# High and low activations side by side: 512 moving columns into two halves of a bank in the third mixer and the cross attention

## The reference

```python
h = rms_norm_2(x, g_mix[i])
q, k, v, z, xbc, dt_raw = jnp.split(h @ w_in[i], splits, axis=-1)
attn = dilated_attention(...q, k, v...)           # 16 heads of 64
ssm = ssd_mixer(z, xbc, dt_raw, ...)              # conv, silu, chunked scan, gate
x = x + jnp.concatenate([attn, ssm], axis=-1) @ w_out[i]
...
q = (h @ w_q)                                     # 4 heads of 128
kv = (mem_h @ w_kv)                               # keys and values of 256 memory rows
p = jax.nn.softmax(jnp.einsum('bshd,bmhd->bhsm', q, k), axis=-1)
```

## Time and profile before

| | |
|---|---|
| median of 3 runs | 3293.85 us (3293.05 to 3294.2) |
| the profiled execution, its own time | 3295.74 us |
| its span in the profile | 3293.9 us |
| PE, matmuls busy | 3277.0 us, 99% of the span |
| DVE busy | 2168.9 us, 66% |
| ACT busy | 1543.6 us, 47% |
| third mixer and cross attention, from its first piece to its last | 2014.8 to 2549.7 us of the span |

### The profile page before, as it was taken

The page is one execution under the profiler, slowest core; times in us unless marked ns, Lnnn a source line. Parts: engine busy times, 40 slices in busy tenths (PEclk is TensorE's granted clock), DMA queues, the critical chain, the costliest instruction groups (busy, mean ns, idle before and its releaser), DMA issues.

```text
span 3293.9 us, 40488 instructions
## 1 busy us (share of the span) xinstructions
PE 3277.0 (99%) x16298; PEld 2765.5 (84%) x16298; DVE 2168.9 (66%) x1803; ACT 1543.6 (47%) x1550; POOL 188.7 (6%) x272
## 2 busy tenths in 40 slices
PE   8999999999999999999999999999999999999999
PEld 7888888888888888888888888999889888888887
DVE  6565777777676565776777676577776555555555
ACT  6645444443445654444444445347554534444443
POOL 0101000000000000000000000000030000000000
PEclk9999999999999999999999999999999999999999
DMA  7456777777755445867777754444354455555554
GB/s 282 154 179 226 267 261 252 249 251 260 254 198 196 171 167 210 276 242 268 252 252 247 263 201 164 154 141 143 140 204 147 173 192 191 186 185 189 191 191 166
DMA packets 106523, 686.28 MB, mean 208 GB/s; under 512 B 14065, under 2 KB 16145, under 8 KB 29617
## 3 DMA queue, kind: packets, MB, share of 16 engines
q1 hardware_dynamic: 84128, 591.43, 50.0%
q0 software_dynamic: 22288, 93.31, 9.2%
HBM read 640.81 MB, written 2.10 MB: 195 GB/s over the span
## 4 chain that ended last, share of the span: by engine, by line
PE 98%; DVE 1%; DMA 1%; ACT 0%; issue 0%; POOL 0%; DVEq 0%
PE ps L528 27%; PE ps L530 27%; PE ps L529 27%; PE ps L496 3%; PE ps L497 3%; PE ps L498 3%; PE ps L550 2%; DVE w_lo L1765 1%; PE ps L633 0%; PE ps L622 0%; PE ps L678 0%; DMA gain_rows_sb<-in_gain_rows 0%; PE ps L592 0%; PE ps L899 0%; PE ps L910 0%; PE ps L949 0%
## 5 line engine op out<-in xcount | busy, mean ns | idle before, releaser
L1187 ACT ACTIVATE w_hi<-w_raw 128x2048 fp32r<-128x2048 f32 x558 | 1067.7, 1915 | 1231.2 <-DMA w_raw<-in_weights 1231.0
L1765 DVE TENSOR_TENSOR w_lo<-w_raw,w_hi 128x2048 fp32r<-128x2048 f32 x558 | 1277.3, 2296 | 480.3 <-ACT w_hi L1187 477.6
L528 PE MATMUL ps<-w_hi,actb_hi 128*128 128x512 f32 x1920 | 749.2, 390 | 0.0
L530 PE MATMUL ps<-w_lo,actb_hi 128*128 128x512 f32 x1920 | 747.1, 389 | 0.0
L529 PE MATMUL ps<-w_hi,actb_lo 128*128 128x512 f32 x1920 | 747.0, 389 | 0.0
L528 PE MATMUL ps<-w_hi,h_hi 128*128 128x512 f32 x1216 | 474.9, 391 | 0.0
L530 PE MATMUL ps<-w_lo,h_hi 128*128 128x512 f32 x1216 | 473.2, 389 | 0.0
L529 PE MATMUL ps<-w_hi,h_lo 128*128 128x512 f32 x1216 | 473.1, 389 | 0.0
L1845 DVE TENSOR_TENSOR x_stream<-x_stream,ps 128x1024 f32<-128x1024 f32 x160 | 195.4, 1221 | 348.9 <-PE ps L530 346.4
L530 PEld LDWEIGHTS ps<-w_lo,actb_hi 128*128 128x128 f32 x1920 | 360.4, 188 | 74.9
L528 PEld LDWEIGHTS ps<-w_hi,actb_hi 128*128 128x128 f32 x1920 | 360.5, 188 | 73.9
(11 more groups left out here) (380 smaller groups left out, 3137.8 us busy)
## 6 DMA issues: line engine op xcount, KB each, us to landing
w_raw<-in_weights SPq DMA_DIRECT2D x558, 1024.0 KB, 4.8
gate_rows<-in_conv_rows POOLq DMA_DIRECT2D x20, 1024.0 KB, 4.9
up_rows<-in_conv_rows POOLq DMA_DIRECT2D x20, 1024.0 KB, 8.9
gate_prev<-gate_tokens POOLq DMA_DIRECT2D x20, 508.0 KB, 5.6
gate_next<-gate_tokens POOLq DMA_DIRECT2D x20, 508.0 KB, 6.8
up_prev<-up_tokens POOLq DMA_DIRECT2D x20, 508.0 KB, 5.7
up_next<-up_tokens POOLq DMA_DIRECT2D x20, 508.0 KB, 6.8
w_raw<-in_weights SPq DMA_DIRECT2D x4, 512.0 KB, 8.3
```

The lines of the kernel that those rows point to most:

```text
L528: mm(o, a_hi, hi, start=first and c == 0, stop=False)
L530: end = mm(o, a_hi, lo, start=False, stop=last and c == 3)
L1187: A(w_hi[:, s], w_raw[:, s], ACT.Identity).then_inc(hi_done, 1)
L1765: tt(w_lo[:, s], w_raw[:, s], hi_of(w_hi[:, s]), ALU.subtract).then_inc(w_ready, 1)
```

## The change

The high and low parts of an activation chunk lie side by side (`acts[:, c, 0]` and `acts[:, c, 1]`), so that one matmul moves both, 512 columns, past the high weights. It fills both halves of a bank: high times high in the left half, high times low in the right one. The third product, low weights times high activations, has 256 columns and is added to the right half. A chunk takes two matmuls where it took three. ACT copies the right half to SBUF (`low_half`), and DVE adds the left half to it and then multiplies by the norm factors. The order on ACT and DVE stays as it was apart from that, except that one `silu_z` and one `tick` change places at the end of the mixer. The first two layers use the new layout with their old instructions.

```diff
-        act_hi = fixed("act_hi", [KC, T], F32R)
-        act_lo = fixed("act_lo", [KC, T], F32R)
+        acts = fixed("acts", [KC, 2, T], F32R)
+        act_hi, act_lo = acts[:, :, 0], acts[:, :, 1]
...
             def wide(p, w, s, pairs, ready=None, chunks=range(KC)):
...
-                    mm(o, hi, acts[0][:, c], start=c == 0, stop=False)
-                    mm(o, hi, acts[1][:, c], start=False, stop=False)
-                    last = mm(o, lo, acts[0][:, c], start=False, stop=c == KC - 1)
+                    mm(ps[:, s, :], hi, pairs[:, c], start=c == 0, stop=False)
+                    last = mm(ps[:, s, T:2 * T], lo, pairs[:, c, 0], start=False, stop=c == KC - 1)
...
+            def low_half(p, s, dst):
+
+                act.wait_ge(acc_done, p + 1)
+                A(dst, ps[:, s, T:2 * T], ACT.Identity).then_inc(low_copied, 1)
...
             def piece2(m):
+                low_half(P_IN2 + m, m % 4, proj[:, m])
                 tick(P_IN2 + m, m % 4)
...
             def evac_scaled(p, s, dst, factors=rstd):
 
-                dve.wait_ge(acc_done, p + 1)
-                tt(dst, ps[:, s, 0:T], factors, ALU.mult).then_inc(acc_free, 1)
+                w = p - P_IN2 if p < P_OUT2 else W_KV + p - P_KV
+                dve.wait_ge(low_copied, w + 1)
+                tt(dst, ps[:, s, 0:T], dst, ALU.add).then_inc(halves_summed, 1)
+                dve.wait_ge(halves_summed, w + 1)
+                tt(dst, dst, factors, ALU.mult).then_inc(acc_free, 1)
```

More of the change, by code:

```diff
@@ L147, in build @@
         proj = arena
-        actb_hi = at("actb_hi", [KC, T], F32R, AR)
-        actb_lo = at("actb_lo", [KC, T], F32R, AR + 16 * KB)
+        actsb = at("actsb", [KC, 2, T], F32R, AR)
+        actb_hi, actb_lo = actsb[:, :, 0], actsb[:, :, 1]
         cst1 = at("consts1_sb", [NJ], F32, AR + 32 * KB)
@@ L260, in build @@
         acc_free = sem("acc_free")
+        low_copied, halves_summed = sem("low_copied"), sem("halves_summed")
         act_hi_done = sem("act_hi_done")
@@ L484, in _, with wide @@
             A_IN, B_IN = (act_hi, act_lo), (actb_hi, actb_lo)
-            def wide(p, w, s, acts, ready=None, chunks=range(KC)):
+            def wide(p, w, s, pairs, ready=None, chunks=range(KC)):
                 pe.wait_ge(w_ready, p + 1)
                 pe.wait_ge(acc_free, w + 1)
-                o = ps[:, s, 0:T]
                 for c in chunks:
@@ L508, in opening @@
                         turn()
-                    wide(p + s, w + s, s, A_IN, ready if s == 0 else None, range(8))
+                    wide(p + s, w + s, s, acts, ready if s == 0 else None, range(8))
                 for part in range(8, KC, 4):
                     for s in range(3):
-                        wide(p + s, w + s, s, A_IN, ready if s == 0 else None, range(part, part + 4))
+                        wide(p + s, w + s, s, acts, ready if s == 0 else None, range(part, part + 4))
             def factor_row(n):
@@ L1026, in piece2 @@
             def piece2(m):
-                wide(P_IN2 + m, W_IN2 + m, m % 4, A_IN)
+                wide(P_IN2 + m, W_IN2 + m, m % 4, acts)
                 steps(m)
@@ L1031, in _ @@
             factor_row(0)
-            wide(P_IN2 + 3, W_IN2 + 3, 3, A_IN)
+            wide(P_IN2 + 3, W_IN2 + 3, 3, acts)
             dt_products()
@@ L1053, in _ @@
             pe.wait_ge(added, S_CO - 1)
-            wide(P_KV, W_KV, 0, B_IN, ready=A0 + 2 * KC)
+            wide(P_KV, W_KV, 0, actsb, ready=A0 + 2 * KC)
             total_pairs(7, SU0 + 10)
-            wide(P_KV + 1, W_KV + 1, 1, B_IN)
+            wide(P_KV + 1, W_KV + 1, 1, actsb)
             pe.wait_ge(added, S_CO)
@@ L1060, in _ @@
             x_quarter(1, S_CO, A0 + 3 * KC)
-            wide(P_KV + 2, W_KV + 2, 2, B_IN)
+            wide(P_KV + 2, W_KV + 2, 2, actsb)
             x_quarter(2, S_CO, A0 + 3 * KC + 4)
-            wide(P_KV + 3, W_KV + 3, 3, B_IN)
+            wide(P_KV + 3, W_KV + 3, 3, actsb)
             x_quarter(3, S_CO, A0 + 3 * KC + 8)
-            wide(P_CQ, W_CQ, 0, A_IN, ready=A0 + 3 * KC)
+            wide(P_CQ, W_CQ, 0, acts, ready=A0 + 3 * KC)
             factor_row(1)
             per_head(S0 + 5, ps[0:16, 6, 0:T], sq3[:, 4:8], 4)
-            wide(P_CQ + 1, W_CQ + 1, 1, A_IN)
-            wide(P_CQ + 2, W_CQ + 2, 2, A_IN)
+            wide(P_CQ + 1, W_CQ + 1, 1, acts)
+            wide(P_CQ + 2, W_CQ + 2, 2, acts)
             pe.wait_ge(rows_ready, 3)
             spread(dtf, 4, range(4))
-            wide(P_CQ + 3, W_CQ + 3, 3, A_IN)
-            wide(P_CV, W_CV, 0, B_IN)
+            wide(P_CQ + 3, W_CQ + 3, 3, acts)
+            wide(P_CV, W_CV, 0, actsb)
             pe.wait_ge(squares_ready, S0 + 6)
@@ L1090, in _ @@
             last.then_inc(scores_ready, 1)
-            wide(P_CV + 1, W_CV + 1, 1, B_IN)
-            wide(P_CV + 2, W_CV + 2, 2, B_IN)
+            wide(P_CV + 1, W_CV + 1, 1, actsb)
+            wide(P_CV + 2, W_CV + 2, 2, actsb)
             def value_turned(c, bank, col):
@@ L1109, in _ @@
             value_turned(1, 0, 2).then_inc(vT_ready, 1)
-            wide(P_CV + 3, W_CV + 3, 3, B_IN, chunks=range(8))
+            wide(P_CV + 3, W_CV + 3, 3, actsb, chunks=range(8))
             pe.wait_ge(negmax_ready, B0 + 5)
@@ L1113, in _ @@
             value_turned(2, 1, 0).then_inc(vT_ready, 1)
-            wide(P_CV + 3, W_CV + 3, 3, B_IN, chunks=range(8, KC))
+            wide(P_CV + 3, W_CV + 3, 3, actsb, chunks=range(8, KC))
             pe.wait_ge(probsT_copied, B0 + 5)
@@ L1636, in _ @@
             A(wdt_hi[:, 256:], wdt_sb[:, 0:112], ACT.Identity).then_inc(wdt_hi_done, 1)
+            for m in range(2):
+                low_half(P_IN2 + m, m % 4, proj[:, m])
             for m in range(2, 16):
@@ L1643, in _ @@
                 piece2(m)
+            tick(P_OUT2, 0)
             silu_z(7)
-            tick(P_OUT2, 0)
             y2 = proj[:, XBC2:XBC2 + 8]
@@ L1676, in _ @@
             x_squared(4, 3, S_CO)
+            act.wait_ge(x_summed, LAYERS * SUMMED + 11)
+            low_half(P_KV, 0, pr3[:, 4])
             tick(P_KV + 1, 1)
             root_of(N0 + 4)
+            low_half(P_KV + 1, 1, pr3[:, 5])
             tick(P_KV + 2, 2)
@@ L1682, in _ @@
             x_root_of(4)
+            low_half(P_KV + 2, 2, pr3[:, 6])
             tick(P_KV + 3, 3)
             x_hi(16, 2, act_hi, cross_gain)
+            low_half(P_KV + 3, 3, pr3[:, 7])
             tick(P_CQ, 0)
@@ L1688, in _ @@
             A(sq3[:, 4:8], pr3[:, 4:8], ACT.Square).then_inc(squares_ready, 1)
+            low_half(P_CQ, 0, pr3[:, 0])
             tick(P_CQ + 1, 1)
             root_of(N0 + 5, slice(0, 16))
+            low_half(P_CQ + 1, 1, pr3[:, 1])
             tick(P_CQ + 2, 2)
+            low_half(P_CQ + 2, 2, pr3[:, 2])
             tick(P_CQ + 3, 3)
+            low_half(P_CQ + 3, 3, pr3[:, 3])
             tick(P_CV, 0)
@@ L1695, in _ @@
             A(sq3[:, 0:4], pr3[:, 0:4], ACT.Square).then_inc(squares_ready, 1)
+            low_half(P_CV, 0, pr3[:, 8])
             root_of(N0 + 6, dst=qf2[:, 1, 0:8], src=qf2[:, 0, 0:8])
             tick(P_CV + 1, 1)
+            low_half(P_CV + 1, 1, pr3[:, 9])
             softmax_exps(B0 + 4, s_x[:, 0], soft[:, 0])
             softmax_scaled(B0 + 4, s_x[:, 0], soft[:, 0])
+            low_half(P_CV + 2, 2, pr3[:, 10])
             tick(P_CV + 2, 2)
             copy_probs(B0 + 4, 4, pt3[:].rearrange("p a b t -> p (a b) t"))
+            low_half(P_CV + 3, 3, pr3[:, 11])
             tick(P_CV + 3, 3)
```

## The result

The changed kernel takes 3317.39 us (median of 4 runs, 3315.47 to 3323.78) against 3294.02 for the one before. The ratio is 1.0073 with a 95% interval of 1.006 to 1.0085: slower by 23.4 us. The profiled execution has a span of 3316.0 us, 22.1 more than before.

The account below looks back on a forecast made before the run. PE, busy for 99% of the span, was taken to bound the kernel. Waits of 27.1 us less 12.8 saved gave + 14.3, so 3308 us against 3293.85, with a range of 3296 to 3320.

Parts of the forecast that it names:

- What PE saves: All 960 chunks: two matmuls for three save 0.0133 us each, 12.8 us of PE's stream.
- 0.6 us of room: Plain pieces: `w_lo` ends at E + 4.95, PE needs it at E + 5.55, so no wait.
- Place 1: Rotation tables, m = 7: late splits make PE wait 3.6 us for piece 10, 0.38 before; + 3.2 us.
- Place 2: Squares, m = 16: `sq_q` ends at E + 4.5, where PE asks at E; + 4.5 us.
- Place 3: Values, m = 26: copy of the first probabilities 2.9 us later, against slack of 1.3; + 2.7 us.
- Place 4: Third softmax, m = 33: scaling 2.9 us later, against slack of 0.4; + 3.4 us.
- Place 5: `xdt`, m = 40: ready at E + 12.55, where PE asks at E + 7.3; + 5.3 us.
- The six that I had not: Smaller hand-overs: dt, values' copy, fourth softmax, decays, two in the cross attention; say 1.3 us each, + 8.
- The clock: Rival, 0.20: PE's clock falls to half in the new waits, 5 to 9 us more, 3313 to 3317.
- Half of the waits: Rival, 0.14: streams give back half the delay, 13 of waits against 12.8; 3294 to 3300, no change.
- Few waits: Rival, 0.10: PE's old slack at the hand-overs takes up the 2.0 us delay; faster, 3284.
- No saving from the widths: Rival, 0.08: the load of weights bounds the short matmul, a piece stays at 5.76 us; 3319.

Follow-up runs that it names:

- widths alone: Changed kernel with three matmuls of 256 columns a chunk put back, its two halves and order kept: 3323.72 us.
- order alone: Kernel before with ACT's copy where the change put it, result overwritten, and DVE waiting for it; matmuls and DVE's work as before: 3322.41 us.
- DVE alone: Changed kernel with ACT in its old order and without the copy; DVE copies, adds and multiplies: 3295.56 us.
- filled waits: Changed kernel with 66 extra matmuls of 512 columns, whose result nobody reads, ahead of five of PE's waits: 3309.77 us.
- splits first: Changed kernel with ACT splitting weights ahead of its copy in the mixer: 3311.93 us; with squares (m = 16) and root (m = 40) also ahead: 3305.57 us.

## Why the prediction was right, and where it was off

It said 3308 us, 3296 to 3320, slower with 0.76. Slower it is, inside the range, but the 23.4 us are 9 more than the 14.3 of the sum, which was made of two terms too large and one that was zero. That the saving (6 us too large) and the waits (8 too large) nearly made up for each other is luck.

- **What PE saves: 12.8, measured 6.3 (timed) to 7.3 (rest), by the kernel that undoes the widths alone,** and 6.2 by the table with the hidden part of the waits. The sign and the alternation were right. The step that failed is "one constant of 13 ns fits both widths". At 2.4 GHz 768 columns are 0.320 us, so the chunk's 0.353 leaves 17 ns for each of the two matmuls, and its 0.346 leaves 13. With 14 pieces of 58 at the one and the others at the other, 16 chunks each, it is 14 x 16 x 0.014 + 44 x 16 x 0.007, some 8 us. What sets the speed of a piece stays open. The rule of the Trainium skill's page "TensorE: Matmul & The Clock Gate", section "Back-to-back issue gap", 2.5 ns for a matmul beside its columns, which the page gives for an isolated one, would make the saving 2.4 us. The traces have 13 to 17 ns in these streams, and don't agree with it.
- **The order as the cost: right, and shown** by the kernel with the order alone (+28 us with nothing saved) and, from the other side, by DVE alone (22 us less with more instructions). The 0.6 us of room in plain pieces held. The changed kernel's timelines give the new rhythm at m = 11, whose next piece starts at 2099.77:

```profile
2099.97 0.39 ACT L1523 ACTIVATE arena<-ps 128x256 f32<-128x256 f32 x1 [3.36 <-PE ps L497]
2100.25 1.91 ACT L1186 ACTIVATE w_hi<-w_raw 128x2048 fp32r<-128x2048 f32 x1
```

```profile
2100.39 0.42 DVE L1853 TENSOR_TENSOR arena<-ps,arena 128x256 f32<-128x256 f32 x1 [1.45 <-ACT arena L1523]
2100.85 0.42 DVE L1855 TENSOR_TENSOR arena<-arena,factors 128x256 f32<-128x256 f32 x1
2102.20 2.29 DVE L1786 TENSOR_TENSOR w_lo<-w_raw,w_hi 128x2048 fp32r<-128x2048 f32 x1 [0.92 <-ACT w_hi L1186]
```

  With E, the end of the piece, at 2099.77, `w_lo` ends at E + 4.7, where I had 4.95.
- **The waits: 27.1, measured 19.4.** Place 1: + 3.2, measured 2.7 less 0.4. Place 2: + 4.5, measured 4.1. Place 3: + 2.7, measured 2.7. Place 4: + 3.4, measured 2.5. Place 5: + 5.3, measured 5.3, in two parts, 1.3 ahead of m = 40 and 4.0 at m = 41. There the last to come was not `xdt` but the silu of the last convolution, which had a table load in front of it. ACT's rows, then DVE's:

```profile
2337.06 1.28 ACT L1550 ACT_TABLE_LOAD   x1
2338.35 0.42 ACT L1550 ACTIVATE arena<-conv_tmp 128x256 f32<-128x256 f32 x1
```

```profile
2326.98 0.15 DVE L1792 TENSOR_SCALAR token_factors<-ps 128x2 f32<-128x2 f32 x1
...
2335.73 2.28 DVE L2354 TENSOR_TENSOR xdt<-ps,dt_tokens 128x2048 f32<-128x2048 f32 x1
```

  `xdt` was ready at 2338.0, the silu at 2338.8. So that place 5 came out at 5.3 is luck in part: neither the 1.3 for DVE's first step nor the silu was in the forecast. The five places that I followed sum to 16.9 against 19.1. The six that I had not, at "1.3 each, say", were to give 8 and gave 2.5 (1.1 for dt, 0.65 for the fourth softmax, 1.2 in the cross attention, less 0.5 that a wait in the output projection lost). This guess is the term of the waits that failed.
- **The clock: 0 in the sum, 6.7 measured.** It was a rival (0.20, 5 to 9 us on top), and it came true along with the likeliest case: falls behind three waits, and a longer one at m = 16. The time of 3317.4 is at the top of that rival's 3313 to 3317. The filled waits show the cause: with the idle time of five waits filled, the falls behind three of them were gone and the kernel was 7.6 us faster. The step that failed is that I priced the waits as idle time alone. The Trainium skill's section "HAM oscillation" on the same page says that idle gaps between bursts of matmuls lower the clock. The trace agrees for these three waits, of 2.7 to 4.0 us.
- **The other rivals.** Half of the waits: they came to 19.4 of the 27.1, and as the saving was halved too, the kernel still got slower. Few waits: refuted in this order, and near to true with the old order on ACT (3295.56), where 6.6 us of new waits and the smaller saving kept it from being faster. No saving from the widths: refuted by the chunk's 0.346 and 0.353 us where it had 0.360, and by the 6.3 us.

What is not settled: in the two kernels with narrow matmuls and the new order the rest is 1.6 and 2.5 us above that of before, with the same matmuls. The 0.16 us that each listed wait leaves out make up 1.1 and 1.3 of it (7 and 8 waits more than before); what is left, 0.5 and 1.2 us, stays open.

## What to carry to other kernels

An engine that runs ahead of the bottleneck carries more than its share of busy time shows: one short instruction that waits for the bottleneck's last result, put at the head of each round, takes the lead from everything behind it. Put such work on an engine that waits there already, even if that one is busier, and use the cheaper form only in rounds that have slack. When waits appear on TensorE, price the slow clock behind them too: in the changed kernel it was a third of their length, and in the other orders between nothing and about half.

## What the runs showed of the hardware that I had not expected

- Of the falls to half clock (0.50, so 1.2 GHz) some belong to a place and some don't: behind the waits for `pt` (2.7, 2.3 and 2.3 us) and for the group products (4.0) they stood in all three kernels that had both (changed, widths alone, order alone); behind that for `w_lo` only in the changed one, with 2.7 us, and not in the other two, with 2.5. Yet both kernels with the splits first had it there, with 2.5, and of the two executions of DVE alone, with 1.9, only the second had. So the length of a wait doesn't decide it. Of these two executions the first lost 6.8 us, at m = 16 and 19, and the other 3.4, behind two waits of 1.9 and 2.2. One profile doesn't settle a difference of 3 us.
- A stream that alternates 512 and 256 columns has two cadences, 0.346 and 0.353 us for the two, and kept the one it had through a run of pieces more often than not. With three matmuls of 256 there was only one, 0.359 to 0.360.
- A multiplication of 128x256 on DVE that waits for the addition just ahead of it started 0.46 us after it (2100.39 to 2100.85, above). Where nothing is waited for, the next instruction starts sooner than that, within the 0.42 us that the first is shown to take. In the kernel before it is 0.34 us behind an evacuation that started at 2089.87:

```profile
2090.21 2.28 DVE L1765 TENSOR_TENSOR w_lo<-w_raw,w_hi 128x2048 fp32r<-128x2048 f32 x1
```

  So the wait for the engine's own last result costs some 0.12 us.
